# Modulation and z's projection in one block: x loaded last, rotary tables loaded by ScalarE and formed early

## The reference, cut to what matters

```python
mod = (jax.nn.silu(cond) @ lw['w_mod'] + lw['b_mod'])[:, None, :]
sh1, sc1, g1, sh2, sc2, g2 = jnp.split(mod, N_MOD, axis=-1)
h = rmsnorm(x, lw['norm1_g']) * (1 + sc1) + sh1
z = h @ lw['w_in']                 # here the first 1984 columns: q_a, k_a, v_a, c_q, c_kv, k_r
qa = rmsnorm(q_a.reshape(b, s, H_A, HD_A), lw['gqa_qn'])   # likewise ka, kr
qa = apply_rope(qa, *rope_a)       # latent tokens only: x * cos and swapped x * sin
```

## Time and profile before

| | us |
|---|---|
| Median of 3 runs | 1730.48 (1727.18 to 1730.88) |
| Profiled execution, own time | 1729.09 |
| Its span in the trace | 1727.3 |
| Modulation's matmuls (L309) | 8.34 to 38.7 |
| First matmul of z (L467) | 52.48 |
| Turn behind unit 5, from which the pace is even | 98.97 |
| Busy over the whole span: PE, DVE, ACT, POOL | 1551.4, 1016.0, 724.5, 652.3 |

### The profile page before, as it was taken

How to read it: one execution, slowest core, us unless ns; L and a number is a source line. 1 busy time by engine, 2 the same in 40 slices (tenths; PEclk the granted TensorE clock), 3 DMA queues, 4 the chain that set the end, 5 groups by cost and what they waited for, 6 DMA issues and landing times. The chain is left out here.

```text
span 1727.3 us, 22786 instructions
## 1 busy us (share of the span) xinstructions
PE 1551.4 (90%) x7699; PEld 1169.3 (68%) x7699; DVE 1016.0 (59%) x1595; ACT 724.5 (42%) x1067; POOL 652.3 (38%) x727
## 2 busy tenths in 40 slices
PE   7799788799989999999896999999999999999992
PEld 2678687688879989964443766666666666666671
DVE  1966687666675565526643665555555555555554
ACT  2422343333442122202213565555555555555560
POOL 0445275322213233300452454344443434444561
PEclk9899899999999999999998999999999999999996
DMA  9320100000035464544174999999999999999954
GB/s 323 100 91 10 37 1 1 1 1 2 1 99 147 140 213 135 146 163 147 59 283 180 335 363 365 353 343 338 352 347 351 343 338 340 339 330 335 344 188 185
DMA packets 130282, 352.66 MB, mean 204 GB/s; under 512 B 22165, under 2 KB 77849, under 8 KB 103193
## 3 DMA queue, kind: packets, MB, share of 16 engines
q1 hardware_dynamic: 98488, 237.87, 37.8%
q10 hardware_dynamic: 10288, 71.86, 11.2%
q0 software_dynamic: 21440, 42.08, 9.7%
HBM read 335.53 MB, written 48.32 MB: 222 GB/s over the span
## 5 line engine op out<-in xcount | busy, mean ns | idle before, releaser
L2289 DVE TENSOR_TENSOR e_wlo<-mem,e_whi 128x2048 fp32r<-128x2048 f32 x140 | 314.6, 2289 | 98.6 <-ACT e_whi L2224 98.6
L2224 ACT ACTIVATE e_whi<-mem 128x2048 fp32r<-128x2048 f32 x140 | 260.2, 1913 | 24.4 <-DMA mem<-in_w_e 16.9
L2194 PE MATMUL psum<-mem 128*128 128x512 f32 x560 | 252.1, 593 | 2.1 <-ACT mem L2256 2.1
L2174 PE MATMUL psum<-e_whi,e_xhi 128*128 128x512 f32 x560 | 228.2, 408 | 7.1 <-DVE e_xlo L2296 7.1
L2176 PE MATMUL psum<-e_wlo,e_xhi 128*128 128x512 f32 x560 | 222.2, 397 | 0.0
L2175 PE MATMUL psum<-e_whi,e_xlo 128*128 128x512 f32 x560 | 222.0, 396 | 0.0
L2132 POOL TENSOR_TENSOR held<-nhalf 1x1 f32<-1x1 f32 x206 | 116.7, 567 | 261.3 <-DMA sums<-mem,si 104.4
L2194 PEld LDWEIGHTS psum<-mem 128*128 128x128 f32 x560 | 101.1, 190 | 103.0 <-issue 102.9
L1494 POOL TENSOR_TENSOR w_lo<-mem,w_hi 128x1024 fp32r<-128x1024 f32 x30 | 76.1, 2560 | 163.6 <-ACT w_hi L1438 163.6
L2296 DVE TENSOR_TENSOR e_xlo<-psum,e_xhi 128x512 fp32r<-128x512 f32 x140 | 90.2, 686 | 76.7 <-ACT e_xhi L2230 76.7
L2306 DVE TENSOR_TENSOR mem<-mem,psum 128x256 f32<-128x256 f32 x70 | 42.5, 607 | 151.0 <-ACT mem L2263 151.0
(11 more groups left out here) (320 smaller groups left out, 3272.8 us busy)
## 6 DMA issues: line engine op xcount, KB each, us to landing
mem<-in_w_e SPq DMA_DIRECT2D x144, 1024.0 KB, 12.3
mem<-in_w_e ACTq DMA_DIRECT2D x66, 1024.0 KB, 11.2
mem<-in_w_mod SPq DMA_DIRECT2D x24, 1024.0 KB, 12.0
mem<-in_w_in SPq DMA_DIRECT2D x16, 512.0 KB, 4.5
mem<-in_w_in SPq DMA_DIRECT2D x3, 2048.0 KB, 8.8
sums<-mem SPq DMA_DIRECT2D x10, 512.0 KB, 4.7
mem<-sums SPq DMA_DIRECT2D x10, 512.0 KB, 5.4
mem<-in_x_sample SPq DMA_DIRECT2D x8, 512.0 KB, 11.0
```

The source lines that it names most:

```text
L2174: pe.matmul(out, xh, wh, start=first, stop=False)
L2194: mm = pe.matmul(pY[:, cs], gT[:, f, :], w2[v][:, f, cs], start=(f == 0), stop=(f == 1))
L2224: act.activation(wHi13[u % 2][:, a], w13[u][:, a], ACT.Copy).then_inc(se["h13"], 1)
L2289: dve.tensor_tensor(wLo13[u][:, a], w13[u][:, a], wHi13[u % 2][:, a].bitcast(F32), ALU.subtract)\
```

## The change

The first block's code becomes functions (`start_sync`, `load_gains`, `start_pool`, `start_rstd`, `take_mod`, `square_rows`, `shift_upper`, `start_cols`, `scale_rows`, `start_mod`, `shift_lower`, `turn_rows`, `start_tensor`) that the second block calls, so the two are one block without a join. SP loads w_mod first, then z's first chunk in two halves with a semaphore each, then x; it loads the second chunk once the modulation's matmuls are done and x is squared. ScalarE issues the loads of gains and tables. x is transposed into banks 4 to 7 in place of 0 to 3; w_mod's chunks trade places in memory, so that z's first high parts can be written once chunks 0 and 1 are used. The reciprocal root is formed tile by tile. `start_tensor` ends with the transposes of x tiles 0 and 1. The split of z's first chunk shares its eight remainders 5 to 3 between VectorE and GpSimd (before 4 to 4).

```diff
-    wmod = [mem.at(M_OA + 4096 * b, KT, 512) for b in range(4)]
+    wmod = [mem.at(M_OA + 4096 * b, KT, 512) for b in (2, 3, 0, 1)]
...
+    def start_sync(sp):
...
         for c in range(4):
             if c > 0:
                 load_mod(c, 0)
             load_mod(c, 1)
+        sp.dma_start(wz[0][:, 0:4, :], w_in_v[:, 0:4, 0:512]).then_inc(s_wz[0], 16)
+        sp.dma_start(wz[0][:, 4:KT, :], w_in_v[:, 4:KT, 0:512]).then_inc(s_wzh, 16)
+        sp.dma_start(xt[:, 0, :], I["x_prompt"][0]).then_inc(s_x[0], 16)
+        for t in range(1, NT):
+            sp.dma_start(xt[:, t, :], I["x_sample"][0, (t - 1) * P:t * P, :]).then_inc(s_x[t], 16)
+        sp.wait_ge(s_mod1, 4)
+        sp.wait_ge(s_sqx, NT)
...
+    def start_rstd(pool, t):
+        pool.wait_ge(s_sqx, t + 1)
...
+    def turn_rows(pe, t):
+        pe.wait_ge(s_xs, t + 1)
+        if t == 1:
+            pe.wait_ge(s_A1, 1)
+        if t >= 2:
+            pe.wait_ge(s_xeV, t - 1)
+            pe.wait_ge(s_xeA, t - 1)
...
+            start_tensor(pe)
             for i in range(n):
                 project(i)
+                if i == 0:
+                    turn_rows(pe, 2)
+                    turn_rows(pe, 3)
                 if i == 1:
+                    turn_rows(pe, 4)
                     turn_cache()
...
             def rows_hi(t):
+                shift_upper(act, t)
+                act.wait_ge(s_xeV, t + 1)
+                act.wait_ge(s_xeA, t + 1)
...
-            rows_hi(0)
-            weights_hi(0, 0, KT)
-            rows_hi(1)
+            load_gains(act)
+            take_mod(act, 0)
+            take_mod(act, 1)
+            weights_hi(0, 0, 4)
+            take_mod(act, 2)
+            weights_hi(0, 4, KT)
+            square_rows(act, 0)
+            square_rows(act, 1)
+            take_mod(act, 3)
+            rows_hi(0)
+            square_rows(act, 2)
+            rows_hi(1)
+            for t in (3, 4):
+                square_rows(act, t)
+            for t in (2, 3):
+                rows_hi(t)
...
-                if i + 2 < NT:
-                    rows_hi(i + 2)
                 squares(i)
                 if i == 1:
+                    rows_hi(4)
...
-            weights_lo(0, range(1, KT, 2))
+            start_pool(pool)
+            weights_lo(0, (1, 3, 5))
+            for t in range(NT):
+                start_rstd(pool, t)
...
+            start_cols(dve)
             dve.wait_ge(s_gain, 16 * 12)
             dve.wait_ge(s_tabs, 16 * 4)
-            rows_lo(0)
-            for k in range(0, KT, 2):
+            tables(CqA, CkA, CqA, gA, HD, SCALE_A)
+            tables(SqA, SkA, SqA, gA, HD, SCALE_A)
+            tables(CqB, CkB, CqB, gB, ROPE, SCALE_B)
+            tables(SqB, SkB, SqB, gB, ROPE, SCALE_B)
+            dve.sem_inc(s_gd, 1)
+            for n, k in enumerate((0, 2, 4, 6, 7)):
                 dve.wait_ge(s_wh, k + 1)
...
-            rows_lo(1)
-            tables(CqA, CkA, CqA, gA, HD, SCALE_A)
-            tables(SqA, SkA, SqA, gA, HD, SCALE_A)
+            for t in range(2):
+                scale_rows(dve, t)
+            start_mod(dve)
+            shift_lower(dve, 0)
+            shift_lower(dve, 1)
+            rows_lo(0)
+            scale_rows(dve, 2)
+            rows_lo(1)
+            scale_rows(dve, 3)
+            scale_rows(dve, 4)
+            for t in (2, 3):
+                shift_lower(dve, t)
+                rows_lo(t)
             for i in range(n):
-                if i + 2 < NT:
-                    rows_lo(i + 2)
                 sums(i)
+                if i == 1:
+                    shift_lower(dve, 4)
+                    rows_lo(4)
                 if i >= 1:
                     apply(i - 1)
                 if i == 2:
-                    tables(CqB, CkB, CqB, gB, ROPE, SCALE_B)
-                    tables(SqB, SkB, SqB, gB, ROPE, SCALE_B)
-                    dve.sem_inc(s_gd, 1)
                     dve.wait_ge(s_cc0, 1)
```

More of the change, by code:

```diff
@@ L188, in __call__ @@
             self.eng.wait_ge(self.s, self.n)
[L191 to L322, removed]
-                    tr = pe.transpose(bank(2 * (t % 2), 2)[:, k * P:(k + 1) * P],
-                                      xt[:, t, k * P:(k + 1) * P], ident[:, :])
-                tr.then_inc(s_xT, 1)
@@ new lines, in xbank, with take_mod, square_rows, shift_upper @@
+    def xbank(t):
+        return bank(4 + 2 * (t % 2), 2)
+    def take_mod(act, c):
+        act.wait_ge(s_mod1, c + 1)
+        act.activation(modr[:, c, :], bank(c)[0:2, :], ACT.Copy).then_inc(s_modr, 1)
+    def square_rows(act, t):
+        act.wait_ge(s_x[t], 16)
+        if t:
+            act.wait_ge(s_sqx, t)
+        act.activation(sqd, xt[:, t, :], ACT.Square, accum_out=ss[:, t:t + 1]).then_inc(s_sqx, 1)
+    def shift_upper(act, t):
+        y = min(t, 1)
+        act.wait_ge(s_A1, 3)
+        act.wait_ge(s_xT, t + 1)
+        for k in range(4, 8):
+            ins = act.activation(hT[:, k, t * P:(t + 1) * P], xbank(t)[:, k * P:(k + 1) * P], ACT.Identity,
+                                 bias=modc[:, k, y:y + 1], scale=A1[:, k, y:y + 1])
+        ins.then_inc(s_xeA, 1)
@@ new lines, in start_mod @@
+    def start_mod(dve):
+        dve.wait_ge(s_modT, 1)
+        bias = cols[:, 16:32].unsqueeze(2).to_broadcast([P, 16, 2])
+        dve.tensor_tensor(modc[:, 0:16, :], pm[:, 0:16, :], bias, ALU.add).then_inc(s_A1, 1)
+        dve.wait_ge(s_A1, 1)
+        dve.tensor_scalar(A1, modc[:, 8:16, :], 1.0, None, ALU.add).then_inc(s_A1, 1)
+        dve.wait_ge(s_A1, 2)
+        gain = cols[:, 64:72].unsqueeze(2).to_broadcast([P, KT, 2])
+        dve.tensor_tensor(A1, A1, gain, ALU.mult).then_inc(s_A1, 1)
+        dve.wait_ge(s_A1, 3)
@@ new lines, in shift_lower @@
+    def shift_lower(dve, t):
+        y = min(t, 1)
+        dve.wait_ge(s_xT, t + 1)
+        for k in range(4):
+            ins = dve.tensor_scalar(hT[:, k, t * P:(t + 1) * P], xbank(t)[:, k * P:(k + 1) * P],
+                                    A1[:, k, y:y + 1], modc[:, k, y:y + 1], ALU.mult, ALU.add)
+        ins.then_inc(s_xeV, 1)
+    def turn_rows(pe, t):
[5 more added lines that the diff above has]
+            pe.wait_ge(s_xeA, t - 1)
+        for k in range(KT):
+            tr = pe.transpose(xbank(t)[:, k * P:(k + 1) * P], xt[:, t, k * P:(k + 1) * P], ident[:, :])
+        tr.then_inc(s_xT, 1)
@@ new lines, in start_tensor @@
+    def start_tensor(pe):
+        pe.wait_ge(s_const, 16)
+        pe.wait_ge(s_silu, 1)
+        pe.transpose(bank(6)[:, 0:84], rows[0:84, :], ident[0:84, 0:84]).then_inc(s_rowsT, 1)
+        pe.wait_ge(s_cols, 1)
+        for c in range(4):
+            for k in range(KT):
+                if k % (KT // 2) == 0:
+                    pe.wait_ge(s_wm[2 * c + min(k, 1)], 16)
+                mm = pe.matmul(bank(c)[0:2, :], cols[:, k:k + 9:8], wmod[c][:, k, :],
+                               start=(k == 0), stop=(k == KT - 1))
+            mm.then_inc(s_mod1, 1)
+        for c in range(4):
+            pe.wait_ge(s_modr, c + 1)
+            for j in range(4):
+                tr = pe.transpose(pm[:, 4 * c + j, :], modr[:, c, j * P:(j + 1) * P], ident[0:2, 0:2])
+        tr.then_inc(s_modT, 1)
+        turn_rows(pe, 0)
+        turn_rows(pe, 1)
```

70 lines of the change are left out of this document (66 added, 4 removed).

## The result

The changed kernel is slower: 1744.12 us (median of 4 runs, 1740.59 to 1744.38) against 1729.87 for the kernel before on the same chip, ratio 1.008, 95% interval [1.0063, 1.0098]. The forecast was 1724.2, with a range of 1718 to 1731. The profiled execution took 1740.59, its span is 1739.0.

A forecast was written before the change was run, and what follows sets the result against it. TensorE was taken to set the pace, delayed by z's late start and table operations. Earlier start +5.5, waits and slow unit +8.1, transposes -3.3, new wait -3.6, slow unit -2.0, rest +0.9: 5.6 us gained, 1724.2, range 1718 to 1731.

The forecast's parts named there:

- Step 2: Start of z as the tables put it: last table's landing, taken as 30 us, plus 16.8; with semaphores 47.0.
- first rival: The two load queues alternate packet for packet: last table lands at 35, z starts at 51.9, time 1728.8; chance 0.17.
- Step 1: Start of z as x puts it: x0 lands near 37.0 us, last modulation row copied by 40.2, z starts at 46.5.
- Step 3: z's units 0 to 5: TensorE waits 3.6 us before unit 0's transpose, unit 3 costs 7.6, unit 5 ends at 93.4.
- Turns packet for packet: The first rival: each small packet waits for one of 2 KB, gain only 0.7 us, time 1728.8; chance 0.17.
- ScalarE's issues stuck: ScalarE's gain and table issues caught in SP's stall: last table lands at 41, z starts at 58, 1734.5 us; chance 0.08.

The follow-up runs named there:

- the divided kernels: Changed kernel, table operations in their old places, ScalarE issuing only the 4 tables or only the 12 gains, SP the rest: stage end 186.09 and 190.19 us.
- the run with wide rows: Changed kernel with the four table loads read as 128 long rows each in place of 640 short ones: 1735.22 us.
- both halves undone: Changed kernel with gains and tables loaded by SP behind x and table operations in their old places: 1723.57 us, 0.998 of the kernel before.

## Why the prediction was wrong

**Step 2 failed, by L, and set the start of z.** I took the last table's landing at 30, with 44 as its high end; it was 48.0. From there the step's own formula held: L + 16.8 = 64.8, and z started at 65.52 (L + 17.5). Three errors are in L. The first is the argument that set aside the turns. In the earlier trace rows one queue moved 95 packets and the other 39, and I read it as a share in a contest. It says only what both queues moved in 3 us: from 996 to 998 us the same two queues moved 5 and 94, the other way round. Why they differ there no run shows; from 15 to 39 us of the changed kernel, with both queues full, nothing like it occurs. Worked out with even turns, my own first rival gave 35. The second error is in that too: it counted 256 packets of each engine at 104 ns from 8.5 us. The queue carried 4352 / 16 = 272, pairs went at about 107 ns where nothing held them (16 x 3 us / 450), and the first packet of ScalarE's queue moved only between 10.5 and 11 us, though its first load was issued at 6.99: 29.1 us from 10.5 give 39.6. The third error is the pauses that the gains make, 7.2 us by the divided kernels: 46.8. The last 1.2 us fit the 4 KB rows of x, beside which a pair takes 138 ns (16 x 2 us / 232, from 40 to 42 us). This sum is an estimate. For the kernel with the tables alone on ScalarE it gives 10.5 + 164 x 0.107 = 28.0, and there the last table landed at 29.7.

**Step 1 failed, by x0, in the cost of a small packet.** Said: x0 there at 37.0, the last modulation row's copy done by 40.2. Measured: x0 landed at 44.0 and squared at 44.63, the copy ending at 47.5. z's weights, ahead of x, were late as well: ScalarE began its high parts at 39.22 (said: 31). And the premise that the modulation keeps its pace failed by a wait of 1.01 us for w_mod. (x's rows are 4 KB, not 2: from 43 to 44 us SP's queue moved 105 packets, 0.39 MB.) I charged a small packet 18 ns of an engine, 4.6 us for 4096. For the tables that is about right (3.2 us for 2560 rows, 20 ns each; with them alone on ScalarE x0 is squared at 37.40). For the gains it is 7.2 us for 1536, 75 ns each. The earlier trace rows could not have given this. Its 355 packets, all under 512 bytes, are gains; the share gives 15 ns of an engine's work for each, the time that passed 16 us / 355 = 45 ns, and the window is the mean of a half with 296 packets and a nearly empty one with 59. For the 827 packets of tables the share gives 24 ns and the time 39. So the share was far too low for the gains, and the time that passed too high for the tables. What was missing is a row of both queues at once. Even without the table operations in VectorE's way, this alone would have put z at 54.8 (9.5 us behind x0, just the distance of step 1), not at 46.5: with late table operations the kernel ends its stage at 194.05, slower than before.

**Step 3 held in kind.** Said: a wait of 3.6 us before the first turn and a slow unit 3. Measured: 5.06, and unit 3 at clock 0.50 in 7.8 us (said 7.6); then 0.49 before the third turn. Unit 0 took 7.2 (said 8.2). From z's start to the turn behind unit 5 it was 47.6 us, said 46.4. That error is 1.2 us; the start of z made 18.5.

**The rivals.** "Turns packet for packet" had the right mechanism and too small a price, because it left x at step 1's time and knew no pauses. "ScalarE's issues stuck" had the right sign and came nearest (z at 58, 1734.5 us, against 65.5 and 1744.12), but that is luck: ScalarE's last issues did stall (6.76 and 5.43 us), yet its queue moved packets from 10.5 us on, and the last table then needed 22.6 us to land. It was said to decide from L = 35.7 on; by the step's own numbers the tables' path overtakes x's (46.5) from L = 29.7 on, and 35.7 is where z would start no earlier than before. Had L been 30 as said, the forecast would still have been wrong: in the run with wide rows L was 34.6, and x set z's start at 54.71. The early wait at the head of VectorE's queue was given no cost of its own, since with L = 30 it ended just where x's path did (46.8 against 46.5). With x in time it costs 17.2 us, since the last table lands at 47.9 even from SP's queue behind x.

**What was right.** The reading that the first 130 us are all that matters and that every later stage moves with them; that one block can be worth something (both halves undone: 0.998, and 0.9945 with x early and VectorE lighter, though no run takes the join out alone); the marks that would prove the forecast wrong (L over 34, a wait for w_mod, unit 5 ending later than 96), which all three came true.

## What to carry to other kernels

A load on a second queue isn't a load in a free lane: its packets and the first queue's went one for one here, so a thousand short rows beside a stream of large ones cost the stream time, and if they are slow ones, much of it. Don't put a wait at the head of an in-order queue unless its data is there before anything behind it is wanted; here one such wait for small tables held back the scaling of x by 11 us. And don't price small packets beside a stream from a window in which their queue ran alone: by its busy share a gain packet was worth 15 ns, and beside the stream it cost 75.

## What the runs showed of the hardware that was not expected

- 12 loads that each read one short vector for 128 partitions, on ScalarE's queue beside SP's stream, halve the stream for several us (189 GB/s at share 0.62, 358 at 1.09 with the tables in their place). Reading 128 different rows of the same size out of w_in they cost x 1.1 us and not 7.2.
- SP's and ScalarE's queues move equal numbers of packets, within 2 in 3 us (471 to 469, 243 to 244), through a twofold change of pace.
- Each of these loads adds 16 packets to its rows: 4096 + 16 x 16 = 4352 on ScalarE's queue, 1536 + 12 x 16 = 1728 with gains alone.
- ScalarE's first load was issued at 6.99 us, and its queue's first packet moved between 10.5 and 11, beside a full SP queue.
- The same loads issued by GpSimd took most of the engines' time: from 10 to 15 us the DMA share is 1.09 with only 181 GB/s moved, and GpSimd's queue alone has 0.63 of it for 0.15 MB.
